# Hybrid trunk step: states moved into the gaps ahead of the experts, the last two couples' stages reordered, and x summed with their shares in PSUM

## The reference

```python
x = _layernorm(DEEPNORM_ALPHA * x + mix, ln1_g[l], ln1_b[l])
ple = jax.nn.sigmoid(x @ w_ple_gate[l]) * (p[l] @ w_ple_proj[l])
logits = (xt @ w_router_l + b_router_l).astype(jnp.float32)
top_v, top_i = lax.top_k(logits, TOP_K)          # 4 of 32 experts
gates = jax.nn.softmax(top_v, axis=-1)
# for each block of rows of one expert
gate = jnp.minimum(xb @ wg[e] + bg[e], SWIGLU_LIMIT)
up = jnp.clip(xb @ wu[e] + bu[e], -SWIGLU_LIMIT, SWIGLU_LIMIT)
glu = gate * jax.nn.sigmoid(gate * SWIGLU_ALPHA)
y_rows = ((up + 1.0) * glu) @ wd[e] + bd[e]
# y[token] = sum over its rows of gate * y_row
x = _layernorm(DEEPNORM_ALPHA * x + ffn + ple, ln2_g[l], ln2_b[l])
```

## Time and profile before

| | |
|---|---|
| median of 3 runs | 1250.95 us |
| the profiled execution: its own time | 1253.7 us |
| its span, first to last instruction | 1251.8 us |
| PE busy | 1169.6 us (93%) |
| DVE busy | 357.2 us (29%) |
| ACT busy | 186.4 us (15%) |
| DMA | 442.18 MB, 353 GB/s on average |
| granted TensorE clock, mean | 0.976 |

### The profile page before, as it was taken

How to read it: one execution, slowest core, us unless ns; L and a number is a source line. 1 busy time by engine, 2 the same in 40 slices (tenths; PEclk the granted TensorE clock), 3 DMA queues, 4 the chain that set the end, 5 groups by cost and what they waited for, 6 DMA issues and landing times.

```text
span 1251.8 us, 13175 instructions
## 1 busy us (share of the span) xinstructions
PE 1169.6 (93%) x5601; PEld 485.4 (39%) x5601; DVE 357.2 (29%) x568; ACT 186.4 (15%) x346; POOL 69.7 (6%) x74
## 2 busy tenths in 40 slices
PE   5999999899999997899999999999999999998985
PEld 4678775633333332243333333332323232322221
DVE  6866334531313130111222222122212121213014
ACT  2444342311001010020201000010101010110000
POOL 3100141110101030000000000000000000000000
PEclk9999999699999998999999999999999999999988
DMA  9652130689999999999999999999999999999892
GB/s 313 215 151 68 68 139 19 264 350 380 420 421 421 421 418 386 420 421 422 416 421 420 421 421 421 405 421 421 420 421 421 419 422 413 421 421 421 357 421 86
DMA packets 70509, 442.18 MB, mean 353 GB/s; under 512 B 7952, under 2 KB 8368, under 8 KB 21296
## 3 DMA queue, kind: packets, MB, share of 16 engines
q1 hardware_dynamic: 65600, 425.66, 83.5%
q0 software_dynamic: 4848, 15.64, 3.7%
HBM read 436.54 MB, written 4.73 MB: 353 GB/s over the span
## 4 chain that ended last, share of the span: by engine, by line
PE 73%; DMA 17%; DVE 7%; ACT 2%; issue 1%; SPq 1%; DVEq 0%
PE ps L1011 42%; DMA ring<-in_w_up 12%; PE ps L593 9%; PE ps L992 6%; DMA ring<-in_w_gate 4%; PE ps L944 3%; DVE y_s L1883 3%; PE ps L814 2%; DVE h_s L1881 2%; PE ps L999 2%; PE ps L621 1%; ACT hTe L1162 1%; PE ps L1027 1%; PE ps L976 1%; PE ps L948 1%
## 5 line engine op out<-in xcount | busy, mean ns | idle before, releaser
L1011 PE MATMUL ps<-ring,xTe 128*64 128x512 f32 x1536 | 358.1, 601 | 17.7 <-DMA ring<-in_w_up 14.5
L1011 PEld LDWEIGHTS ps<-ring,xTe 128*64 128x64 f32 x1536 | 105.5, 136 | 242.4 <-issue 242.2
L1011 PE MATMUL ps<-ring,hTe 128*64 128x512 f32 x768 | 180.8, 610 | 7.1 <-DMA ring<-in_w_down 7.1
L1863 DVE TENSOR_TENSOR xs<-xs,ps 128x512 f32<-128x512 f32 x64 | 44.0, 688 | 348.5 <-PE ps L992 348.4
L593 PE MATMUL ps<-xT,ring 128*128 128x288 f32 x448 | 115.4, 414 | 1.0 <-PE ps L593 0.6
L1011 PE MATMUL ps<-more,xTe 128*64 128x512 f32 x496 | 113.5, 599 | 1.6 <-DMA more<-in_w_up 0.8
L1011 PEld LDWEIGHTS ps<-ring,hTe 128*64 128x64 f32 x768 | 52.3, 139 | 121.8 <-issue 121.4
L593 PEld LDWEIGHTS ps<-xT,ring 128*128 128x128 f32 x448 | 84.8, 193 | 25.3 <-issue 2.3
L992 PE MATMUL ps<-y_s,GT 128*128 128x512 f32 (+1 forms) x256 | 82.5, 520 | 2.2 <-ACT y_s L1162 1.2
L1881 DVE TENSOR_SCALAR h_s<-ps 128x512 f32<-128x512 f32 x32 | 21.8, 681 | 161.0 <-PE ps L1011 161.0
L1162 ACT ACTIVATE h_s<-g_s 128x1024 f32<-128x1024 f32 x16 | 16.9, 1056 | 307.7 <-DVE g_s L1871 307.7
(11 more groups left out here) (371 smaller groups left out, 817.8 us busy)
## 6 DMA issues: line engine op xcount, KB each, us to landing
ring<-in_w_gate SPq DMA_DIRECT2D x96, 1024.0 KB, 11.2
ring<-in_w_up SPq DMA_DIRECT2D x96, 1024.0 KB, 11.7
ring<-in_w_down SPq DMA_DIRECT2D x96, 1024.0 KB, 13.6
more<-in_w_gate SPq DMA_DIRECT2D x32, 1024.0 KB, 9.9
more<-in_w_down SPq DMA_DIRECT2D x32, 1024.0 KB, 13.0
more<-in_w_up SPq DMA_DIRECT2D x30, 1024.0 KB, 13.1
ring<-in_w_in SPq DMA_DIRECT2D x28, 512.0 KB, 6.2
ring<-in_w_out SPq DMA_DIRECT2D x8, 512.0 KB, 5.1
```

What stands on the lines that cost most here:

```text
L1011: last = mm(ps[64 * q:64 * q + 64, bank0 + half, :], lhs(k, q), wide(t)[:, k % 2, half * 512:(half + 1) * 512], start=False, stop=k == KT - 1)
L1863: tt(x, x, ps[:, CB_BANKS[n], 0:512 if i < 2 else QW], ALU.add).then_inc(S["cb_added"], 1)
```

## The change

**Head.** On PE `prompt_states_b` moves from behind the sample ranks to between the statistics of the sample tile and its transposes. On DVE the wait for `kbt_mm` moves from ahead of the norm of tile 1 to its last instruction, and on ACT the square root of that norm moves ahead of the copies of the keys. `select` is split in two: for tile 0 the norm of the sample tile starts between the halves. The rests that feed the bf16 parts of tile 2 come one place earlier. The first gathers go to banks 7 and 2 instead of 0 and 1, the first gate stage starts after one of two copies to `xTe`, and the gathers of the second couple move from up 0 to gate 0.

The core of the diff:

```diff
+SUM_BANKS = (6, 7, 0, 1, 4)
+STAGES = [(p, w) for p in range(NPAIR - 2) for w in range(3)] + \
+         [(LAST - 1, 0), (LAST - 1, 1), (LAST, 0), (LAST, 1), (LAST - 1, 2), (LAST, 2)]
...
+            def whole_unit(n, whole):
+                return mm(summed(n), ident, unit_of(n), start=True, stop=whole)
+            def last_h(k):
+                if k == 3:
+                    for half in range(2):
+                        h_transposes(LAST, half, half)
+                if k == 5:
+                    pe.wait_ge(S["hTe_ok"], 2 * LAST + 2)
+                if k in (5, 6):
+                    whole_unit(k - 3, False)
...
+            def beside_last_down(k):
+                if 1 <= k <= 5:
+                    if k == 1:
+                        pe.wait_ge(S["y_ok"], LAST)
+                        whole_unit(4, False)
+                    combine_unit(k - 1, GT[(LAST - 1) % 3], SUM_BANKS[k - 1], False, False)
...
-            pe.wait_ge(S["y_ok"], NPAIR)
+            pe.wait_ge(S["y_ok"], NPAIR + 1)
             for n in range(5):
-                if n >= 2:
-                    pe.wait_ge(S["cb_added"], 5 * (NPAIR - 1) + n - 1)
-                combine_unit(n, GT[(NPAIR - 1) % 3])
+                combine_unit(n, GT[LAST % 3], SUM_BANKS[n], False)
             row_stats(3)
...
-            copy_y(NPAIR - 1)
+            copy_y(LAST - 1)
+            act.wait_ge(S["cb_mm"], 5 * LAST)
+            act.wait_ge(S["y_mm"], 4 * LAST + 2)
+            f(y_s[:, 0:512], ps[:, 2, :], ACT.Copy).then_inc(S["y_ok"], 1)
...
-            add_shares(NPAIR - 1, tile_stats)
+            dve.wait_ge(S["cb_mm"], 5 * LAST)
+            dve.wait_ge(S["y_mm"], 4 * LAST + 4)
+            nc.vector.tensor_copy(y_s[:, 512:D], ps[:, 3, :]).then_inc(S["y_ok"], 1)
+            for n in range(5):
+                dve.wait_ge(S["cb_mm"], 5 * NPAIR + n - 4)
+                step(summed_stats(n))
             spread_stats()
...
-            dve.wait_ge(S["kbt_mm"], 1)
             norm(1, 5)
...
-            for n in range(2):
-                gather(xTe[0], 4 * n, 4, n, 0, 128)
+            for n in range(2):
+                gather(xTe[0], 4 * n, 4, ROW_BANKS[n], 0, 128)
```

More of the change, by code:

```diff
@@ L403, in _ @@
                 ring_load(w_out[k], False)
-            for p in range(NPAIR):
-                for t, (w, k, q) in enumerate((w, k, q) for w in range(3) for k in range(KT // 2) for q in range(2)):
-                    t += p * PER
+            for stage, (p, w) in enumerate(STAGES):
+                for t, (k, q) in enumerate((k, q) for k in range(KT // 2) for q in range(2)):
+                    t += stage * KT
                     wide_free(t)
@@ L919, in _ @@
             row_stats(2)
+            prompt_states_b()
             transpose_normed(2)
@@ L925, in _ @@
             sample_ranks()
-            prompt_states_b()
             prompt_states_a()
@@ L990, in combine_unit, with products @@
                 for half in halves:
-                    for out, c in columns(i, half, CB_BANKS[n]):
-                        last = mm(out, gt[:, t0:t0 + r], y_s[:, c], start=True, stop=True)
+                    for out, c in columns(i, half, bank):
+                        last = mm(out, gt[:, t0:t0 + r], y_s[:, c], start=first, stop=last_one)
                 last.then_inc(S["cb_mm"], 1)
-            def products(p, first, bank0, lhs, w, sel_p, after_k, done):
+            def products(p, bank0, lhs, w, sel_p, after_k, done):
                 for half in range(2):
@@ L1001, in products @@
                 for k in range(KT):
-                    tiles = [(p if isinstance(p, int) else NPAIR) * PER + first + 2 * (k // 2) + q for q in range(2)]
+                    first = STAGES.index((p, w)) * KT if isinstance(p, int) else NPAIR * PER + w * KT
+                    tiles = [first + 2 * (k // 2) + q for q in range(2)]
                     if k % 2 == 0:
@@ L1042, in beside_gate @@
                         gates_to_rows(7)
+                elif p == LAST:
+                    if k == 1:
+                        for half in range(2):
+                            h_transposes(LAST - 1, half, 4 + half)
                 elif 1 <= k <= 5:
@@ L1072, in beside_up @@
             def beside_up(p, k):
-                if p == 0 and k in (1, 3):
-                    pe.wait_ge(S["OH_ok"], 1)
-                    gather(xTe[0], 2 * (k - 1), 4, 4 + k // 2, 128, 128)
                 if p < GATHERS and k == 5:
@@ L1091, in beside_up @@
                     ple_product(KT, k - 1)
+                if p == LAST and k in (1, 2):
+                    if k == 1:
+                        pe.wait_ge(S["cb_added"], 5 * (LAST - 1))
+                        pe.wait_ge(S["ple_added"], 5 * (KT + 1))
+                        pe.wait_ge(S["sel_ok"], NPAIR)
+                    whole_unit(k - 1, False)
             pe.wait_ge(S["part_ok"], 8)
@@ L1107, in _ @@
                     pe.wait_ge(S["n_ok"], 1)
[L1108 removed]
+                products(p, 2, lhs, 1, sel[p % 2], lambda k: beside_up(p, k), S["up_mm"])
+                if p >= LAST - 1:
+                    continue
                 for half in range(2):
@@ L1141, in _ @@
                         pe.wait_ge(S["sel_ok"], j + (NPAIR + 1))
-                        products(p, 0, 0, x_cols(xTe[0], 0), 0, sel[0], nothing, S["gate_mm"])
-                        products(p, KT, 2, x_cols(xTe[0], 0), 1, sel[0], nothing, S["up_mm"])
+                        products(p, 0, x_cols(xTe[0], 0), 0, sel[0], nothing, S["gate_mm"])
+                        products(p, 2, x_cols(xTe[0], 0), 1, sel[0], nothing, S["up_mm"])
                         for half in range(2):
@@ L1340, in _ @@
             norm_scale(2, 6)
+            part(2, 0)
             part(1, 1)
-            part(2, 0)
             copy_xT(2, 6, 0)
@@ L1439, in _, with tile_stats @@
             nc.vector.memset(eps[:, 2:3], 1.0).then_inc(S["setup"], 1)
-            def tile_stats(i, done=None):
+            def tile_stats(i):
                 x = tokens(i)
@@ L1444, in tile_stats @@
                     last = nc.vector.bn_stats(lns[:, i, q, :], x[:, q * 512:(q + 1) * 512] if i < 2 else x)
-                    (done or step)(last)
+                    step(last)
             def spread_stats():
@@ L1863, in add_shares @@
                     tt(x, x, ps[:, CB_BANKS[n], 0:512 if i < 2 else QW], ALU.add).then_inc(S["cb_added"], 1)
-                    if after and n in (1, 3, 4):
-                        dve.wait_ge(S["cb_added"], p * 5 + (n + 1))
-                        after(i)
             def gate_half(p):
@@ L1882, in up_half @@
                     dve.wait_ge(S["u_ok"], p * 2 + (half + 1))
+                    if isinstance(p, int) and p == LAST and half == 0:
+                        dve.wait_ge(S["ht_mm"], 2 * LAST)
                     stt(by_row(y_s[:, :])[:, 64 * half:64 * half + 64, :], h_s[:, c].rearrange("r (p k) -> r p k", k=KT), 1.0,
@@ L2014, in _ @@
                         add_shares(j + NPAIR)
-                dve.wait_ge(S["cb_added"], extra * 5 + 5 * NPAIR)
-                for i in range(3):
-                    tile_stats(i, lambda last: last.then_inc(S["stats_anew"], 1))
+                for n in range(5):
+                    dve.wait_ge(S["out_mm"], 6 + n + 1)
+                    summed_stats(n).then_inc(S["stats_anew"], 1)
                 dve.wait_ge(S["stats_anew"], 5)
```

99 lines of the change are left out of this document (65 added, 34 removed).

## The result

The changed kernel took 1246.08 us (median of 7 runs, 1244.15 to 1247.53), the kernel before in the same comparison 1252.32 us (1250.07 to 1254.13): ratio 0.9947, 95% interval 0.9936 to 0.9958. That is 0.5% faster. The forecast of 1234.0 was 12 us too low (1.4 of them because the kernel before took 1252.32 here and not 1250.95), and the time lies outside the range of 1227.5 to 1241.0. The profiled execution has a span of 1243.6 us (own time 1245.4) against 1251.8 before: 8.2 us less, where the sum said 16.8.

A forecast was written before the change was run, and what follows sets the result against it. Weight streaming at 420 GB/s was taken to bound the middle, leaving head and tail to gain: head 7.3, order 6.6, copy 0.3, statistics 2.6, together 16.8, so 1250.95 becomes 1234 us; own range 1231 to 1237, whole range 1227.5 to 1241.

The forecast's parts named there:

- the order of the last stages: Tail: gate 15 straight after up 14 removes the 4.3 us DMA pause; products end at 1225.0 instead of 1231.6, gain 6.6.
- Step 1: Head: tile 1's norm no longer waits 2.43 us; x ends at 218.0, PE's transposes start at once at 218.63.
- Step 6: Head: mLSTM states take 3.4 us at half clock, to 236.5, with no wait for OH.
- Step 7: Head: gathers take 3.3 us plus 1.0 for starting at half clock, to 240.8; the 0.69 for the second copy goes.
- the 16 states: Head, step 3: `prompt_states_b` moved into the sample-tile gap takes 2.1 us at full clock instead of 3.78, to 222.9.
- Copy: After the last product: copy of y split in halves takes 0.7 instead of 1.03 us, gain 0.3.
- Statistics: End: from the copy to the last statistics 5.3 us instead of 7.9, with PE's five units setting the pace; gain 2.6.
- Head: From the out-projection to the experts: start at 241.0 instead of 248.34, gain 7.3.
- A: Rival: the clock never falls in the head; experts start at 235.4, gain 12.9, time 1228.5; chance 0.17.
- B: Rival: the head's clock falls as early as before, at 222.3; start 243.8, gain 4.5, time 1236.8; chance 0.20.
- C: Rival: head's gain doesn't reach the end, first tiles' issues or a later pause take its place; 1241.5; chance 0.08.
- D: Rival: PE stays at 1.2 GHz in the last stages; 1271, or near 1253 for half; 0.05 with anything unseen.

The follow-up runs named there:

- sel_early: Experiment 1: changed kernel with DVE making the selector of couple 15 right after the gate half of couple 14; 1238.8 us, ratio 0.9882 to the kernel before.
- experiment 4: Changed kernel with all the head's edits undone, leaving the last stages and the sums; 1251.99 us, ratio 0.9987 to the kernel before.
- head_only: Kernel before with all the head's edits of the diff and nothing else; 1246.36 us, ratio 0.994 to the kernel before.
- sel_again: Same text as sel_early, run once more beside other kernels on the same chip; 1240.55 us, ratio 0.9901 to the kernel before.
- experiments 8 and 9: `prompt_states_b` put back behind the sample ranks, on the changed kernel (8: 1246.01 us) and on sel_early (9: 1242.04 us).
- kbt_back: Changed kernel with DVE's `kbt_mm` wait back ahead of tile 1's norm and ACT's square root behind the key copies; 1248.95 us, ratio 0.9969 to before.
- sel_gath_back: sel_early with the second couple's gathers back in up 0 and the first in banks 0 and 1, experts waiting for both copies; 1241.4 us, ratio 0.9911.
- sel_states_late: sel_early with `prompt_states_b` put back behind the sample ranks; 1242.04 us, ratio 0.9919 to the kernel before.
- units_early: sel_early with two of five identity products of x moved from the last two to the first two steps of down 14; 1238.74 us, ratio 0.989.
- order_sel_again: Same text as order_sel, run once more beside sel_again on one chip; 1243.62 us, ratio 0.9926 to the kernel before.
- order_sel: sel_early without the sums in PSUM: DVE adds all shares as before, the new stage order stays; 1243.89 us, ratio 0.9921 to the kernel before.
- warm: Changed kernel with six dummy identity products on PE while it waits for the selector ahead of gate 15; 1243.35 us, ratio 0.9919 to before.

## Why the prediction was wrong

**The step that failed** is in the order of the last stages: "After up 14 (ended 1150.3) PE goes straight into gate 15, so its first two places are free at 1150.3 + 0.6 + 3.6 = 1154.5 ... the pause of 4.3 us doesn't come". I took the places and the tiles as the only things gate 15 needs. Its bias products also need `sel` of couple 15. It is made on DVE behind h of couple 14 and behind 2.9 us of additions that nobody is in a hurry for. It came 5.87 us after the end of up 14 and took the clock to half with it. Experiment 1 removes only this and is 5.5 to 7.3 us faster (6.5 by the traces); experiment 4 shows that with it the tail's part is worth 1.3 us. The page and the trace of before show no wait for `sel` there, because a down stage covered it. When a stage is taken out from between two others, each wait that the second one has on other engines must be looked up anew, not only the wait that the move is about.

**A term was mis-sized as well.** Even without the wait the order gained less than 6.6: in sel_early the products end 978.9 us after the experts' start, 983.3 before, so 4.4. I put the landing of the last group of down 14 at 1199.9, which is 951.6 after the experts' start of before. The last pair of down 14 was waited for until 1194.36 in sel_early, 953.6 after its start:

```profile
1194.36 1.94 PE L1043 MATMUL ps<-ring,hTe 128*64 128x512 f32 x8 [0.26 <-DMA ring<-in_w_down]
```

```profile
1212.00:1215.00 3.00, 3.00 (x14) 0.78 (x10) 0.00 (x0) 0.00 (x0) 0.00 (x0) 1.00 0.18 66
```

That is 2.0 us of the 2.2. The stream itself is as forecast: the last window of sel_early with traffic puts its end at 1212 + 0.18 x 3 = 1212.5, 971.8 after the start, where I had 1219.9 - 248.34 = 971.6. But I counted back from there by throughput, and took that for the moment at which a waiting PE goes on. The wait in the row ends 2.0 later; why the tile comes later than the throughput says, no run tells. From that wait on the forecast holds: 25.3 us to the end of the products, where I had 1225.0 - 1199.9 = 25.1.

**The head: right in this execution, with some luck.** Forecast start 241.0, measured 241.18; head_only gains 6.9. Step 1 (x of tile 1 at 218.0) was 219.0, since all up to it, the out-projection too, ran 0.9 later in this execution, so from the end of the out-projection the head took 21.6 us where I had 22.4. The luck is in steps 6 and 7. Step 6 has the mLSTM states at 3.4 "at half clock", from a stretch in which the clock had come back at 242.8; they took 4.4 here (233.57 to 238.00) and 4.7 wholly at half clock (sel_again, 233.52 to 238.23). Step 7 has 1.0 for gathers that start at half clock; here they cost nothing more, and 1.9 in sel_again. The two errors cancel in the one group of executions and add up in the other, with the start at 243.46. Of the rest, the waits, the 16 states at 2.03 for 2.1, and the fall of the clock inside route(2) (227.4 for "about 227") came as written. What was wrong is a part of its attribution. I let the move of the states carry much of the gain; experiments 8 and 9 give it 0 to 1.5 us by the medians (0.2 to 3.1 by the starts), kbt_back gives DVE's wait 2.9 (3.9), and sel_gath_back gives the second copy 0.85. The remaining 2 us or so lie in DVE's new order of choice and norm, or in the parts together; no run took these alone. I had said that the states are what brings the clock back, and then moved half of them away from the place where they do.

**The end: right.** Copy 0.3 for 0.3. Statistics 2.9 for 2.6: the last one takes 0.5 behind PE's units, and statistics and the norm's first step from PSUM cost what they cost from SBUF (0.70, and 1.21 to 1.28). 

**The sum again.** Head 7.16 for 7.3, order -2.1 for 6.6, copy 0.3, statistics 2.9 for 2.6. Of the 8.7 missing in the order, 6.5 (985.4 - 978.9) are the selector and 2.2 what was mis-sized, nearly all of it the landing. With the selector early, the time is 1238.8 and 1240.55 in two comparisons.

**The rivals.** A (the clock never falls) was wrong, and so was B (it falls as early as before) for the changed kernel; kbt_back is B, with 245.1 for its 243.8. By B's page of the Trainium skill ("TensorE: Matmul & The Clock Gate", Part 4: PE-mode transpose) transposes don't count as busy work in the way products do. In the changed kernel the clock outlived 1.06 and 0.38 us of them, with 0.40 us of 24-column products and 2.03 us of states between, and in sel_states_late it fell at 224.1, 4.5 us after the end of the out-projection, with transposes, 24-column products, waits and the first 0.5 us of routing between, so the rule is neither shown nor refuted. C named the right kind of loss (the head's gain is kept, and "a later pause takes its place") and its time of 1241.5 was the nearest, but it placed the pause in the first tiles. D's clock came in one group only, not in a stage. I had no rival for a new wait on DVE in the tail, the kind of wait that the new order takes away elsewhere. The share of 0.5 for a sum of four terms that must all hold was too high, and the range's upper end should have held the case in which the largest uncertain term is nothing: 1234 + 6.6 = 1240.6 and beyond.

## What to carry to other kernels

Before reordering stages, list for the first instruction of each stage every semaphore it waits for, and find each producer's place in its own engine's queue; a producer that nobody waited for can be late after the move, here 0.3 us of work for some 6 us of time. Where a wait on PE can't be avoided, count the slower group behind it too: here it cost 2.1 to 3.9 us by the traces, beside 2.6 for the wait itself. Dense products stood just ahead of the last groups of the head in the kernel before; moving half of them away from there gave back part of what the filled gap gained in the executions with the late return of the clock. And one profiled execution of each text isn't enough where the clock decides: two of the same text differed by 2.7 us in one stretch.

## What the runs showed of the hardware

- One text, two starts: in sel_early and sel_again the products from 233.5 to 235.5 stand alike to 0.02 us, and the clock came back at 236.8 or at 242.6. The profiled executions of the new head fall in two groups. Where it had fallen at 226.5 to 228.0 (changed, sel_early, head_only, units_early, order_sel_again) it was back at 236.7 to 238.2, after 10.2 to 10.3 us. Where it had fallen at 225.6 or 225.7 (sel_again, order_sel, warm, sel_gath_back) it was back at 242.6 to 242.8, after 17.0 to 17.1 us. So a fall 1 us earlier went with a return 6 us later, and none of the nine lies between. The Trainium skill ("TensorE: Matmul & The Clock Gate", Part 1) calls the window in which activity is watched free-running, which would fit two discrete outcomes; no run here shows the window itself.
- PE kept busy without a gap at half clock doesn't always raise the clock: in sel_again it ran products from 225.8 to 242.6 without a wait at 1.2 GHz, first 7.7 us of thin ones (32 columns, or 32 rows), then 9 us of states and gathers. Full clock came only behind these.
- Six products of 128x512 with the identity, 5.42 us in all, kept the clock at 1.00 through a wait of 5.9 us (warm); with a wait of that length without them it stood at 0.51 in the window of 1149 to 1152 (changed kernel).
